# Two index tiles' scores moved into the first attention's first step, a third of the top-k marks moved into the second attention, and GpSimd's low halves written in two operations

## The chip, the cores and the metric

The kernel runs on one core of one Trainium2 chip. The metric is device time in microseconds (us), from the median of several executions. TensorE (PE) multiplies, VectorE (DVE) and ScalarE (ACT) work elementwise on SBUF and PSUM, GpSimd (POOL) splits the weights, SyncE (SP) issues the weight loads. TensorE's granted clock has two levels here, 1.2 and 2.4 GHz (1.00 in the profile).

## The reference, cut to what matters

Two transformer-like layers on 512 tokens of width 1024 are followed by a pooling layer, a dilated-attention layer and a final norm. Each of the first two layers has three branches: an mLSTM, a sparse attention (`_dsa`) in which each query may look only at the 128 keys with the highest index score, and a differential attention (`_diff_attn`).

```python
def _dsa(q, k, v, qi, ki, wi):            # per block of queries
    rel = jax.nn.relu(jnp.einsum('bqhd,bsd->bqhs', qib, ki32))       # 4 index heads
    score = jnp.einsum('bqh,bqhs->bqs', wib * idx_scale, rel)
    score = jnp.where(causal[None], score, -jnp.inf)
    _, idx = lax.top_k(score, topk)                                   # topk = 128
    ...
    s = jnp.where(valid[:, None], jnp.einsum('bqhd,bqkhd->bhqk', qb, k_sel) * (dh ** -0.5), -jnp.inf)
    p = jax.nn.softmax(s, axis=-1)

def _diff_attn(q, k, v, lam):
    p = jax.nn.softmax(jnp.where(causal, s, -jnp.inf), axis=-1)
    a = p[:, :, 0] - lam * p[:, :, 1]
```

## The kernel before, in words

All 512 tokens are resident as four tiles of 128 (`NT` = 4). Every engine has its own program, written by hand, and the engines meet only at semaphores. So the order of the text is the order of each engine's queue.

Weights come in 546 chunks of up to 1024 columns through four `RAW` slots. For each chunk GpSimd (`split`, L371 to L382) writes a rounded high half `WH` (L377) and then the rest, `WL` (L380), into one of two slots; `weights_split` tells TensorE that `WL` is complete, and `chunk_done` frees the slot. TensorE multiplies with `WH` and then with `WL` (`by_columns`, L407). The small operation at L376 is the one on which GpSimd waits for a free slot.

In each of the two layers a stretch of mLSTM work is followed by the index scores, and these by two attentions. The index scores (PE L664, ACT's relu in `RELU`, DVE L1713 to L1720) are made for the query tiles n = 1, 2 and 3, four heads each, with 256, 384 and 512 keys; tile 0 needs none. Four PSUM banks (0, 1, 4, 5) carry the heads, two `RELU` buffers pass them to VectorE, and VectorE adds the weighted heads in the tile's part of `MSK`. Only behind the last relu does ScalarE copy the turned keys (`take` into `SKT` and `DKT`) that the first attention's scores wait for.

The attentions are `for a in range(2)`: a = 0 is the differential one, a = 1 the sparse one. Both run nine steps q = 0 to 8; step q makes the scores of tile n = q // 2 for four heads and finishes step q - 1. TensorE's order in a step of a = 0 is: `scores(q)` (L729), `gate_high` (L691, 16 matmuls), `turn_probs(q-1, 0)` (L740), `gate_low` (L699, 8), `values` (L752), `turn_probs(q-1, 1)`, `branch` (L407, 12), `values`. The gate and branch chunks are the weights of the gated merge; they are placed there to fill TensorE. In a = 1 there are four `turn_probs` and `values` a step, the first `values` directly behind `gate_high`.

VectorE's order in a step is: four masked maxima of the scores (L1776) and their negation (L1781), in a = 0 the normalised difference of the probabilities of q - 1 (L1790 to L1797), `use_gate(q-1)` (L1754), `scale_gate(q)` (L1743), then in a = 0 six rounds of `mark_top`, and in every other step a copy of the attention's output (L1815, or L1818 to L1820). A round of `mark_top` takes the eight highest index scores of a tile (L1730) and overwrites them with a marker (L1731). Sixteen rounds do a tile, and L1733 turns the markers into the mask. The 48 rounds of the three tiles fill the steps 0 to 7 of a = 0. The masks are read by L1776 of a = 1: tile 1's at q = 2, tile 2's at q = 4, tile 3's at q = 6.

ScalarE's order in a step is: four exponentials of q, the copies of the turned probabilities of q - 1 to `TB`, and the gate's tanh.

## Time and profile before

| | us |
|---|---|
| median of 3 runs (lowest 3347.69, highest 3351.09) | 3349.46 |
| the profiled execution | 3356.99 |
| its span, first to last instruction | 3354.8 |
| busy: PE / DVE / ACT / POOL | 3094.3 / 1679.1 / 577.0 / 1872.8 |
| mean granted clock of TensorE | 0.969 |

The span is the profiled execution without 2.2 us around it. An engine's busy time is a mean over stages with different limits, so the stages are to be looked at one by one. In the chain of waits each line is the start, the duration and the work that the end of the program waited for; in a timeline a bracket tells how long the engine had stood idle and who released it.

### The profile page before, as it was taken

To read this page: it belongs to the slowest core of one execution; us is meant where nothing else is said; L and a number is where in the kernel's file an instruction comes from. 1 tells how busy PE (TensorE), PEld (TensorE's weight loads), DVE (VectorE), ACT (ScalarE), POOL (GpSimd) and SP (SyncE) were. 2 spreads that over 40 slices of the span, in tenths; PEclk is the share of its full clock that TensorE was granted. 3 is DMA by queue.
4 is the path that set the end of the run, shared out by engine and by line. 5 is a ranking of instruction groups with operands and counts; after the bars stand their busy time and mean duration, and the time that the engine had idled before them with its cause. 6 is when DMAs were issued, how large, how long until landed. Compare 5 with 4: busy or idle time off the path is not lost.

```text
span 3354.8 us, 39077 instructions
## 1 busy us (share of the span) xinstructions
PE 3094.3 (92%) x14414; PEld 2545.1 (76%) x14414; DVE 1679.1 (50%) x2562; ACT 577.0 (17%) x1130; POOL 1872.8 (56%) x1645
## 2 busy tenths in 40 slices
PE   8977889999999987779999999999999999998998
PEld 6866667788877876557778878777778888887876
DVE  6777853554433777773464433555422223323544
ACT  3223233110001331323110000000011211111000
POOL 5643333666667664324566667665565554444664
PEclk9998999999999998889999999999999999999999
DMA  4321111333323321111233323322222222222322
GB/s 137 95 63 42 56 47 54 116 94 94 102 82 114 103 86 54 47 42 57 65 122 97 97 88 95 94 83 92 85 88 76 82 74 67 67 67 66 97 88 75
DMA packets 86524, 272.49 MB, mean 81 GB/s; under 512 B 9984, under 2 KB 10624, under 8 KB 86400
## 3 DMA queue, kind: packets, MB, share of 16 engines
q1 hardware_dynamic: 86400, 270.84, 26.5%
q8 instruction: 78, 1.28, 0.2%
q14 instruction: 46, 0.38, 0.0%
HBM read 266.61 MB, written 4.19 MB: 81 GB/s over the span
## 4 chain that ended last, share of the span: by engine, by line
PE 81%; DVE 14%; ACT 3%; issue 1%; DMA 0%; SPq 0%; POOL 0%; DVEq 0%; ACTq 0%
PE PS L407 54%; PE PS L456 13%; PE PS L699 3%; PE PS L691 3%; DVE MSK L1731 2%; DVE SMALLS L1730 2%; PE PS L927 2%; PE PS L752 1%; PE PS L953 1%; DVE MS L1776 1%; ACT MS L1042 1%; PE PS L740 1%; PE PS L941 1%; PE PS L420 1%; ACT TB L1042 1%
## 5 line engine op out<-in xcount | busy, mean ns | idle before, releaser
L380 POOL TENSOR_TENSOR WL<-RAW,WH 128x1024 fp32r<-128x1024 f32 (+3 forms) x546 | 1229.1, 2251 | 45.5
L376 POOL TENSOR_TENSOR POOL_C<-POOL_C 128x1 f32<-128x1 f32 x546 | 127.7, 234 | 1412.6 <-PE PS L407 776.5
L407 PE MATMUL PS<-XNH,WH 128*128 128x512 f32 x1752 | 694.0, 396 | 14.2 <-DVE EYL L1428 9.1
L407 PE MATMUL PS<-XNL,WH 128*128 128x512 f32 x1752 | 686.5, 392 | 0.0
L377 POOL TENSOR_SCALAR WH<-RAW 128x1024 fp32r<-128x1024 f32 (+3 forms) x546 | 538.2, 986 | 0.5 <-issue 0.5
L407 PE MATMUL PS<-XNH,WL 128*128 128x512 f32 x1752 | 432.9, 389 | 0.0
L407 PEld LDWEIGHTS PS<-XNH,WH 128*128 128x128 f32 x1752 | 330.7, 189 | 87.1 <-DVE EYL L1428 10.3
L407 PEld LDWEIGHTS PS<-XNL,WH 128*128 128x128 f32 x1752 | 330.7, 189 | 69.2 <-issue 1.0
L407 PEld LDWEIGHTS PS<-XNH,WL 128*128 128x128 f32 x1752 | 328.1, 187 | 69.0
L456 PE MATMUL PS<-WH,XNH 128*128 128x512 f32 (+1 forms) x768 | 288.4, 376 | 6.7 <-ACT TB L1042 3.8
L456 PE MATMUL PS<-WH,XNL 128*128 128x512 f32 (+1 forms) x768 | 285.9, 372 | 0.0
L1970 DVE SCALAR_TENSOR_TENSOR OQK<-PS,RT 128x512 f32<-128x512 f32 x48 | 33.1, 692 | 312.9 <-PE PS L407 307.0
L456 PE MATMUL PS<-WL,XNH 128*128 128x512 f32 (+1 forms) x768 | 178.3, 372 | 0.0
L456 PEld LDWEIGHTS PS<-WH,XNH 128*128 128x128 f32 x768 | 145.0, 189 | 28.4 <-ACT TB L1042 4.4
L456 PEld LDWEIGHTS PS<-WH,XNL 128*128 128x128 f32 x768 | 144.7, 188 | 19.6
L456 PEld LDWEIGHTS PS<-WL,XNH 128*128 128x128 f32 x768 | 141.5, 188 | 20.3
L691 PE MATMUL PS<-XNH,WH 128*128 128x512 f32 x384 | 156.5, 408 | 0.0
L691 PE MATMUL PS<-XNL,WH 128*128 128x512 f32 x384 | 151.2, 394 | 0.0
L407 PE MATMUL PS<-HH,WH 128*128 128x512 f32 x352 | 139.5, 396 | 7.3 <-DVE HL L1428 7.3
L407 PE MATMUL PS<-HL,WH 128*128 128x512 f32 x352 | 139.3, 396 | 0.0
L1845 DVE TENSOR_TENSOR HT<-SILU,PS 128x512 f32<-128x512 f32 x44 | 30.3, 688 | 202.1 <-PE PS L407 199.6
L1428 DVE TENSOR_TENSOR HL<-HT,HH 128x512 f32 (+1 forms) x44 | 112.6, 2559 | 5.1
(351 smaller groups left out, 4713.5 us busy)
## 6 DMA issues: line engine op xcount, KB each, us to landing
RAW<-w_oslot SPq DMA_DIRECT2D x56, 512.0 KB, 3.6
RAW<-w_L0ffn SPq DMA_DIRECT2D x44, 512.0 KB, 3.6
RAW<-w_L1ffn SPq DMA_DIRECT2D x44, 512.0 KB, 3.6
RAW<-w_od SPq DMA_DIRECT2D x32, 512.0 KB, 3.6
RAW<-w_epool SPq DMA_DIRECT2D x24, 512.0 KB, 3.6
RAW<-w_oslot SPq DMA_DIRECT2D x32, 384.0 KB, 3.1
RAW<-w_eug SPq DMA_DIRECT2D x16, 512.0 KB, 3.6
RAW<-w_eout SPq DMA_DIRECT2D x16, 512.0 KB, 3.6
```

Of the source, the lines that this page charges most:

```text
L376: nc.gpsimd.tensor_tensor(POOL_C[:, 1:2], POOL_C[:, 0:1], POOL_C[:, 0:1], ALU.add)
L377: nc.gpsimd.tensor_scalar(WH[:, half, 0:w], RAW[:, slot, 0:w], 1.0, 0.0, ALU.mult, ALU.add).then_inc(S("high_ready"), 1)
L380: nc.gpsimd.tensor_tensor(WL[:, half, 0:w], RAW[:, slot, 0:w], WH[:, half, 0:w].bitcast(F32), ALU.subtract).then_inc(S("weights_split"), 1)
L407: mm = nc.tensor.matmul(bank, w[:, slot, k * cols:(k + 1) * cols], x[:, k0 + k, :], start=first and j == 0 and w is WH and x is hi, stop=l ...
L456: mm = nc.tensor.matmul(outs[n], x[:, k, n * P:(n + 1) * P], w[:, slot, j * cols:(j + 1) * cols], start=k == 0 and w is WH and x is hi, st ...
L691: nc.tensor.matmul(PS[b][:, :], WH[:, c % 2, k * P:(k + 1) * P], x[:, k, :], start=k == 0 and x is XNH, stop=False)
L699: mm = nc.tensor.matmul(PS[b][:, :], WL[:, c % 2, k * P:(k + 1) * P], XNH[:, k, :], start=False, stop=k == KD - 1)
L927: nc.tensor.matmul(PS[g][:, 0:(n + 1) * P - k0], OQK[:, half, g, n * P:(n + 1) * P], OQK[:, half, 3 + g, k0:(n + 1) * P], start=True, stop ...
L1042: nc.scalar.activation(out_, in_, func, **more).then_inc(sem, 1)
L1428: V.tensor_tensor(dst_lo, src, dst_hi.bitcast(F32), ALU.subtract).then_inc(sem, 1)
L1730: then(V.max(TOP8, m))
L1731: then(V.match_replace(m, TOP8, m, TAKEN))
```

## The change

1. `mark_top`: in a = 0, four rounds instead of six in each of the steps 0 to 7 (rounds 0 to 31: tiles 1 and 2). The sixteen rounds of tile 3 go to the steps 0 to 3 of a = 1, four in each, at the same place of VectorE's step.
2. Index scores: only tile 1 is made before the attentions. The scores, relus and sums of the tiles 2 and 3 go into step 0 of a = 0: on TensorE behind `gate_low` and ahead of `branch`, with two banks (4, 7) instead of four; on ScalarE behind the exponentials and ahead of the gate's tanh; on VectorE behind the four rounds of marks. `RELU` lies in `TMP` instead of `SQ`, which holds the gates by then.
3. GpSimd writes the low half of a 1024-column chunk in two operations of 512 columns; the second signals. Narrower chunks are as before.

```diff
-        RELU = SQ
+        RELU = TMP
...
-                nc.gpsimd.tensor_tensor(WL[:, half, 0:w], RAW[:, slot, 0:w],
-                                        WH[:, half, 0:w].bitcast(F32), ALU.subtract
+                if w == 1024:
+                    nc.gpsimd.tensor_tensor(WL[:, half, 0:512], RAW[:, slot, 0:512],
+                                            WH[:, half, 0:512].bitcast(F32), ALU.subtract)
+                at_ = 512 if w == 1024 else 0
+                nc.gpsimd.tensor_tensor(WL[:, half, at_:w], RAW[:, slot, at_:w],
+                                        WH[:, half, at_:w].bitcast(F32), ALU.subtract
                                         ).then_inc(S("weights_split"), 1)
...
-                for n in range(1, NT):
+                def index_scores(n, banks):
+
                     w = (n + 1) * P
                     for h in range(IDX_HEADS):
-                        b = (0, 1, 4, 5)[h]
+                        b = banks[h % len(banks)]
                         claim(b)
...
+                index_scores(1, (0, 1, 4, 5))
                 pe.wait_ge(*L("sk_normed", 1))
...
                         if gated:
                             gate_low(name, i)
+                        if a == 0 and q == 0:
+                            index_scores(2, (4, 7))
+                            index_scores(3, (4, 7))
...
-                act.wait_ge(*L("dk_normed", 1))
-                for n in range(1, NT):
+                def index_relu(n, banks):
+
                     for h in range(IDX_HEADS):
                         i = 4 * (n - 1) + h
                         act.wait_ge(*L("idx_ready", i + 1))
                         if i >= 2:
                             act.wait_ge(*L("idx_used", i - 1))
                         w = (n + 1) * P
-                        run(RELU[:, i % 2, 0:w], PS[(0, 1, 4, 5)[h]][:, 0:w], ACT.Relu, L("relu_ready"))
+                        run(RELU[:, i % 2, 0:w], PS[banks[h % len(banks)]][:, 0:w], ACT.Relu, L("relu_ready"))
+
+                act.wait_ge(*L("dk_normed", 1))
+                index_relu(1, (0, 1, 4, 5))
...
+                        if a == 0 and q == 0:
+                            index_relu(2, (4, 7))
+                            index_relu(3, (4, 7))
...
-                for n in range(1, NT):
+                def index_sum(n):
+
...
+
+                index_sum(1)
...
                         if a == 0 and q < 8:
-                            for r in range(6):
-                                mark_top(6 * q + r)
+                            for r in range(4):
+                                mark_top(4 * q + r)
+                        if a == 0 and q == 0:
+                            index_sum(2)
+                            index_sum(3)
+                        if a == 1 and q < 4:
+                            for r in range(4):
+                                mark_top(32 + 4 * q + r)
```

## Rows read from the trace of the kernel before

**Rows 1.** The page: shares of the chain of waits by engine, whole span.

```profile
PE 81%; DVE 14%; ACT 3%; issue 1%; DMA 0%; SPq 0%; POOL 0%; DVEq 0%; ACTq 0%
```

**Rows 2.** Busy time in two stretches (start:end, length, each engine's busy us, granted clock).

```profile
329.00:447.00 118.00, 91.62 (x423) 70.83 (x421) 100.82 (x284) 26.90 (x78) 45.14 (x48) 0.92 0.19 54
...
465.00:581.00 116.00, 107.12 (x582) 84.67 (x581) 35.16 (x106) 35.30 (x97) 45.52 (x48) 0.99 0.19 55
```

**Rows 3.** Chain of waits, first attention: first and last gate scaling, and marks between.

```profile
329.56 0.69 DVE SQ L1743
...
331.14 0.44 DVE SMALLS L1730
...
332.12 0.44 DVE SMALLS L1730
...
402.34 0.71 DVE SMALLS L1730
...
403.85 0.70 DVE SMALLS L1730
...
434.32 0.69 DVE SQ L1743
```

**Rows 4.** Timeline of TensorE, first attention: a short and two long pauses.

```profile
349.71 2.09 PE L699 MATMUL PS<-XNH,WL 128*128 128x512 f32 x8
...
363.95 0.66 PE L740 MATMUL PS<-IDENT,MS 128*128 128x128 f32 x2 [3.91 <-DVE MS L1797]
...
430.17 0.65 PE L740 MATMUL PS<-IDENT,MS 128*128 128x128 f32 x4 [3.76 <-DVE MS L1797]
430.55 3.66 PE L699 MATMUL PS<-XNH,WL 128*128 128x512 f32 x8
```

**Rows 5.** Timeline of TensorE: last gate_high matmul of two steps, first values of one.

```profile
359.65 0.39 PE L691 MATMUL PS<-XNL,WH 128*128 128x512 f32 x1
...
396.63 0.83 PE L752 MATMUL PS<-DV,TB 128*128 128x128 f32 x6
...
406.61 0.39 PE L691 MATMUL PS<-XNL,WH 128*128 128x512 f32 x1
```

**Rows 6.** Timelines of ScalarE and VectorE, index stretch: relus 4 and 12, a load, sums.

```profile
310.97 0.38 ACT L1042 ACTIVATE SQ<-PS 128x256 f32<-128x256 f32 x1 [0.21 <-DVE MSK L1716]
...
316.80 0.60 ACT L1042 ACTIVATE SQ<-PS 128x512 f32<-128x512 f32 x1 [0.26 <-DVE MSK L1716]
...
321.34 1.28 ACT L1042 ACT_TABLE_LOAD   x1
...
312.42 0.42 DVE L1713 TENSOR_SCALAR MSK<-SQ,SMALLS 128x384 f32<-128x384 f32 x1
...
318.46 0.29 DVE L1720 SCALAR_TENSOR_TENSOR MSK<-CAUSAL,MSK 128x128 f32<-128x128 f32 x1
```

**Rows 7.** Timelines, second attention: VectorE's idle stretches; a copy and its reader.

```profile
469.27 0.29 DVE L1776 CUSTOM_DVE_ANT_0 MS<-PS,CAUSAL 128x128 f32<-128x128 f32 x1 [3.54 <-PE PS L729]
...
491.10 0.20 DVE L1818 RECIPROCAL SMALLS<-SMALLS 128x8 f32<-128x8 f32 x1 [3.37 <-PE PS L752]
...
505.02 0.56 DVE L1776 CUSTOM_DVE_ANT_0 MS<-PS,MSK 128x384 f32<-128x384 f32 x1 [5.19 <-PE PS L729]
...
484.08 0.25 ACT L1042 ACTIVATE TB<-PS 128x128 f32<-128x128 f32 x1
...
484.63 0.33 PE L752 MATMUL PS<-X,TB 128*128 128x64 f32 x2
```

**Rows 8.** Timelines of GpSimd and VectorE side by side, at two ends of a stage.

```profile
649.12 2.39 POOL L380 TENSOR_TENSOR WL<-RAW,WH 128x1024 fp32r<-128x1024 f32 x1
649.35 2.71 DVE L1762 SCALAR_TENSOR_TENSOR ML<-TMP,MH 128x512 fp32r<-128x512 f32 x1
...
1063.81 1.05 POOL L377 TENSOR_SCALAR WH<-RAW 128x1024 fp32r<-128x1024 f32 x1
...
1064.03 1.37 DVE L1417 TENSOR_TENSOR X<-X,HT 128x512 f32<-128x512 f32 x1
1064.95 2.68 POOL L380 TENSOR_TENSOR WL<-RAW,WH 128x1024 fp32r<-128x1024 f32 x1
```

## The prediction

> **What bounds the kernel now.** I read the page's chain of waits first. The end of the program waits for TensorE in 81% of the span and for VectorE in 14%, for GpSimd in none [rows 1]. The 14% are not spread evenly, so I went to the busy times by stretch. In the first attention of layer 0 (329 to 447) VectorE is busy 100.8 of 118 us, TensorE 91.6, at a mean granted clock of 0.92; in the second attention (465 to 581) it is the other way round, VectorE 35.2 of 116 us and TensorE 107.1 at 0.99 [rows 2]. So the first attention waits for VectorE, and the second has VectorE to spare. That is the stage to price. The chain there runs in a ring: scaling the gate (L1743), the marks, the maxima, the difference of the probabilities, then TensorE's `turn_probs` and `gate_low`, then L1743 again. The seven rounds of that ring, from the first L1743 at 329.56 to the last at 434.32, take 104.8 us [rows 3]. TensorE's pauses in it end at a VectorE result, L1797 [rows 4]. Layer 1 repeats the picture, so I price one layer and double it.
>
> **The change part by part.** All sums are in the profiled execution, 3356.99 us, which is 7.5 us over the median of the three runs; I take that off at the end.
>
> *Marks out of the first attention.* A round costs the distance between two L1730: 332.12 - 331.14 = 0.98 us over 256 keys and 403.85 - 402.34 = 1.51 over 512 [rows 3]; for 384 keys I take the middle, 1.25. In the seven ring turns VectorE now does rounds 0 to 41: 16 x 0.98 + 16 x 1.25 + 10 x 1.51 = 50.8 us. Afterwards it does rounds 0 to 27: 16 x 0.98 + 12 x 1.25 = 30.7. That is 20.1 us off a stage in which VectorE ends last. The mask step L1733 of tile 2 also moves out of these turns into the tail; I price it like half a round, 0.7.
>
> *What is late next.* With less to do on VectorE, TensorE's own step could bind. For 256 keys it is from `gate_low` at 349.71 to the last `gate_high` matmul at 359.65 and its 0.23, 10.2 us, and 0.2 for the turn: 10.4 [rows 4, 5]. For 512 keys it is 396.63 to 406.84, 10.2 us, then 0.35 of turns and 1.9 of `gate_low`: 12.4 [rows 4, 5]. For 128 keys the same parts are 9.3: 2.8 of `branch`, 0.7 of scores, 3.7 of `gate_high`, 0.2 and 1.9. VectorE's seven turns would be 104.8 - 20.1 - 0.7 - 4.8 (the clock, next) = 79.2 us, 11.3 in the mean, shorter at first and longer at the end, since the maxima and probabilities grow with the keys. So VectorE stays last but in the first turns; I give back 1.2, an estimate.
>
> *The clock.* After a short pause the eight matmuls of `gate_low` take 2.09 us; after a pause of 3.76 they take 3.66 [rows 4], because the engine is then at the lower of its levels, 1.2 instead of 2.4 GHz. There are three such pauses in the ring of layer 0, at 363.95 the first and at 430.17 the last [rows 4]. Shorter marks leave no pause above 1.5 us in the turns 2 to 7, so 3 x 1.6 = 4.8 us come back.
>
> *Index tiles 2 and 3.* Ahead of the attention they are a serial chain. ScalarE's fourth relu ends at 311.35 and its twelfth at 317.40 [rows 6], and the copies of the keys, the scores and everything else follow the last: 6.0 us less. In step 0 they come back. VectorE's eight sums and two causal adds take 318.75 - 312.42 = 6.3 us [rows 6]. The added wait is TensorE's: its last index matmul needs bank 7, which needs the tenth relu, which needs the eighth sum, and that is queued on VectorE behind the gate scaling (0.7) and four rounds (3.9). From L1743 on, this is 0.7 + 3.9 + 2.7 (the first four sums) + 0.6 (a relu [rows 6]) + 0.5 = 8.4 us until `branch(0)` may start; behind it are queued `scores(1)`, `gate_high(1)` and all that the next turn needs. Then follow the 9.3 from above, and one slow start of 1.7 after the long pause. The first turn is then 19.4 us instead of 9.3. So the move costs 10.1 and returns 6.0: it loses 4.1 us. If the clock stays up it loses 2.4. The trace has no relu behind an exponential; if the change of function asks for a table, there and back, each load costs 1.28 as the one at 321.34 [rows 6], 6.7 us lost; I take 0, since the relus of the trace follow a root without one. The chunk of `branch(0)` keeps its slot 8 us longer, so GpSimd's and SyncE's queues stand for as long; no load or split is moved past another, and both are two chunks ahead when they go on.
>
> *The tail.* Behind the last L1743 stand six rounds of 1.51, afterwards four of 1.25 and a mask step: 9.1 - 5.0 = 4.1, less the moved 0.7 but without TensorE in the way, so 3.7.
>
> The first attention with its approach: 20.1 + 0.7 + 4.8 - 1.2 - 10.1 + 6.0 + 3.7 = 24.0 us a layer.
>
> *Marks into the second attention.* Four rounds of 1.51 are 6.0 us, at a place where VectorE has now idle stretches of 3.54 (behind step 0), about 4, 3.37 and 5.19 us before it is wanted again [rows 7]. They overflow by 2.5, 2.0, 2.7 and (with the mask step) 1.3 us. Behind them wait the maxima, behind these ScalarE's exponentials, and in ScalarE's queue behind those the copy to `TB` that TensorE's first `values` reads. The slack there is small: the copy ends at 484.33 and its reader starts at 484.63 [rows 7]. I take 0.3 to 0.5 off in the first two steps and nothing in the others: 2.0 + 1.6 + 2.7 + 1.3 = 7.6, and 0.6 for a chance of the lower clock after the longest pause: 8.2 us a layer. Bounds: 0 if TensorE's order absorbs it all, and 24 if no round is covered.
>
> *GpSimd in two operations.* VectorE's ML took 2.71 us: it came 0.23 behind the low half's start and ended 0.55 after its end at 651.51, so it stood and then worked [rows 8]. And it gets in between two operations: GpSimd's L377 ended at 1064.86, its next one came 0.09 later, and VectorE's L1417, waiting since 1064.03, was through at 1065.40, while that next operation was drawn out to 2.68 [rows 8]. So two halves cut such a wait by some 1.1 us where VectorE's operation is the last before TensorE goes on; in a row of such operations the second waits for the second half and nothing is won. On the path I count three single ones a layer (this one, and at the starts of the two norms): at 1.1, 1.1 and 0.7 that is 2.9 a layer, 5.8 in all. The mLSTM stretch has rows of them: 0, with +-3 either way. GpSimd's own cost rises by an instruction's start, which I bound by the 0.09 between two operations and 0.5: nothing, since nobody waits for it [rows 1]. That cover is gone only where a chunk's split outlasts TensorE's 24 matmuls on the other slot, 24 x 0.23 = 5.5 us; the split is 1.05 + 0.09 + 2.39 and a small operation, some 3.7 [rows 8].
>
> The Trainium skill, SBUF — State Buffer, section "Who interferes with whom", says the shared port pair is an exclusive lock held for the whole instruction, and that a VectorE instruction with two SBUF inputs contends with a reading GpSimd one. Rows 8 agree. By the rule alone, total blocking is not reduced by cutting an operation, only its longest piece is; a row of contending operations would win nothing, and the sum would be 0 instead of 5.8 if every wait were in such a row.
>
> The sum: 2 x (24.0 - 8.2) + 5.8 = 37.4. 3356.99 - 37.4 = 3319.6, less 7.5 gives 3312 us.
>
> **The rivals.**
> - *The marks hide wholly in the second attention* (each step's slack is larger than the one row shows, since `gate_high` runs meanwhile): 16 us more come off, 3296 us. Against it: the 0.3 us in rows 7.
> - *Half the gain of the first attention.* TensorE, or ScalarE's exponentials ahead of the copies, takes VectorE's place in every turn instead of two: 12 a layer are lost, 3336 us. For it: TensorE's 12.4 us in the late turns, close to what VectorE has left.
> - *The gains cancel.* Besides that, the clock drops in each of the four second-attention steps (4 x 1.6 = 6.4 a layer), 2 x (12.0 - 8.2 - 6.4) + 5.8 = 0.6, 3349 us: no difference.
> - *Slower, by one mechanism: the marks in the second attention are fully exposed.* The place is the wait for the maxima; the price is 4 x (6.0 + 1.6 for the clock) + 0.7 = 31 us a layer against 24, so 14 more in all and 3349.5 + 14 - 6 = 3358. It decides from (24.0 + 2.9) / 4 = 6.7 us a step upward. Against it: VectorE's idle stretches are in the trace, 3.4 us and more.
> - *The port's gain is larger*: the stretched waits of the mLSTM stretch are halved as well, some six a layer at 1.1: 3299 us.
> - *It doesn't do what it says*: if tile 3's marks were not done before step 6 reads them the step would wait; they end in step 3, so I give this nothing.
>
> **How the numbers follow.** The forecast, 3312 (3300 to 3326 by its own terms), has 0.55; marks hidden 0.10; larger port gain 0.08; half the gain 0.15; cancelled 0.07; slower 0.05. The range for 8 in 10 takes in both rivals below and half the gain above: 3292 to 3338. A difference of 0.2%, 6.7 us, is about what a measurement of this kernel can tell from none. Faster by more: 0.55 + 0.10 + 0.08 + 0.15 = 0.88; within: 0.07; slower: 0.05.
>
> **What would show it.** In the profile after: L1743 of the first attention some 89 to 92 us from first to last instead of 104.8, with a first turn of 18 to 20 and the others at 10 to 13; granted clock above 0.95 there; the first scores 6 us earlier; TensorE idle 1.3 to 2.7 us before `values` in the steps 1 to 4 of the second attention, released by ScalarE; GpSimd's low halves of 1024 columns gone, ML near 1.6. I am wrong if TensorE waits for GpSimd anywhere, if turns 3 to 7 stay above 14 us, or if the clock falls in the second attention.

## The result and the profile after

The changed kernel takes 3326.15 us (median of 4 runs, 3320.76 to 3331.25), the kernel before in the same comparison 3348.71: a ratio of 0.9922, 95% interval 0.9911 to 0.9934. The medians differ by 22.6 us, the ratio makes it 26 with an interval of 22 to 30; 37.4 was forecast. The kernel is faster, by some 0.7 to 0.8%. The profiled execution took 3326.61, 30.4 less than the one before.

**The chain of waits.** The page of the changed kernel, shares of the span by engine:

```profile
PE 83%; DVE 12%; ACT 3%; issue 1%; DMA 0%; SPq 0%; POOL 0%; DVEq 0%; ACTq 0%
```

VectorE's share went from 14 to 12% [rows 1]. The busy times by stretch say where (start:end, length, busy us of PE, PEld, DVE, ACT, POOL, then the granted clock). The stretches are the first turn of the first attention's ring, its other six turns, and the steps 0 to 3 of the second attention:

```profile
326.06:349.17 23.11, 19.62 (x65) 11.84 (x65) 13.69 (x40) 6.79 (x18) 5.78 (x8) 0.78 0.11 34
349.17:418.93 69.76, 68.50 (x342) 52.93 (x340) 60.08 (x184) 23.26 (x66) 34.63 (x42) 1.00 0.24 68
442.40:505.23 62.83, 53.57 (x251) 41.48 (x250) 41.54 (x107) 18.09 (x60) 23.18 (x28) 0.89 0.17 51
```

In the six other turns TensorE is busy 68.5 of 69.8 us at the full clock. In the kernel before the same six turns took 93.9 us, with TensorE busy in 76.0 of them at 0.91:

```profile
340.44:434.32 93.88, 75.97 (x341) 58.20 (x340) 79.40 (x221) 23.16 (x66) 33.83 (x36) 0.91 0.18 51
```

The price stands in the other two rows of the changed kernel: a first turn of 23 us at a clock of 0.78, and four steps of the second attention at 0.89 (1.00 in layer 1, below).

**The first turn.** Timeline of VectorE, changed kernel; the gate scaling is now L1762, a round of marks L1749 and L1750, an index sum L1730 and L1733, a maximum L1795:

```profile
326.06 0.69 DVE L1762 TENSOR_TENSOR SQ<-PS,RT 128x512 f32<-128x512 f32 x1 [4.66 <-PE PS L706]
...
330.59 0.42 DVE L1730 TENSOR_SCALAR MSK<-TMP,SMALLS 128x384 f32<-128x384 f32 x1
331.12 2.06 DVE L1733 SCALAR_TENSOR_TENSOR MSK<-TMP,SMALLS,MSK 128x384 f32<-128x384 f32 x3
...
335.11 0.75 DVE L1733 SCALAR_TENSOR_TENSOR MSK<-TMP,SMALLS,MSK 128x512 f32<-128x512 f32 x1 [0.80 <-ACT TMP L1052]
...
343.18 0.29 DVE L1795 CUSTOM_DVE_ANT_0 MS<-PS,CAUSAL 128x128 f32<-128x128 f32 x1 [4.23 <-PE PS L736]
```

TensorE in the same stretch (L669 is an index score, two records for each head; L411 is `branch`):

```profile
327.44 1.29 PE L669 MATMUL PS<-X 64*128 64x384 f32 x4 [0.57 <-ACT TMP L1052]
331.65 5.55 PE L669 MATMUL PS<-X 64*128 64x512 f32 x8 [2.91 <-ACT TMP L1052]
337.13 0.79 PE L411 MATMUL PS<-YAH,WH 128*128 128x512 f32 x1
...
342.55 0.71 PE L736 MATMUL PS<-DKT,DQT 64*128 64x128 f32 x8
```

TensorE stands 2.91 us behind the marks, then does tile 3's four heads in 5.55 us, 1.39 a head, at a low clock, and `branch` after them is slow too, 5.42 us from 337.13 to 342.55. VectorE, whose sums should be the slow part, waits between them.

**The second attention.** TensorE's waits before `values` (L759) and one `gate_low` (L706) behind them; VectorE's last round of marks and the maxima behind it; the copy to `TB`:

```profile
455.95 0.66 PE L759 MATMUL PS<-X,TB 128*128 128x64 f32 x2 [2.75 <-ACT TB L1052]
...
456.48 3.76 PE L706 MATMUL PS<-XNH,WL 128*128 128x512 f32 x8
...
485.80 0.97 PE L759 MATMUL PS<-X,TB 128*128 128x64 f32 x4 [2.69 <-ACT TB L1052]
...
502.39 0.66 PE L759 MATMUL PS<-X,TB 128*128 128x64 f32 x4 [1.60 <-ACT TB L1052]
```

```profile
452.11 0.68 DVE L1750 MATCH_REPLACE8 MSK<-SMALLS,MSK 128x512 f32<-128x512 f32 x1
452.82 0.29 DVE L1795 CUSTOM_DVE_ANT_0 MS<-PS,CAUSAL 128x128 f32<-128x128 f32 x1
...
455.55 0.26 ACT L1052 ACTIVATE TB<-PS 128x128 f32<-128x128 f32 x1
```

The maxima have no idle time in front of them now, where [rows 7] had 3.54 us: they start when the marks end. The exponentials, the copy and `values` follow in the order that the prediction named.

Layer 1 has the same pause of 2.75 us at the same place, and there the clock stays up: `gate_low` takes 2.09 us, and the four steps take 59.1 us instead of 62.8. The same steps in the second profile of the kernel before (*before again*, layer 0) are the last row:

```profile
1490.41 0.41 PE L759 MATMUL PS<-X,TB 128*128 128x64 f32 x2 [2.75 <-ACT TB L1052]
...
1490.69 2.09 PE L706 MATMUL PS<-XNH,WL 128*128 128x512 f32 x8
...
1476.73:1535.80 59.07, 48.12 (x251) 36.94 (x250) 41.53 (x107) 18.22 (x60) 23.22 (x28) 1.00 0.18 54
...
465.04:515.53 50.49, 47.68 (x251) 37.10 (x250) 19.01 (x57) 18.28 (x60) 22.57 (x24) 1.00 0.20 63
```

**GpSimd's halves.** GpSimd and VectorE at `ML` (L1781 now):

```profile
640.26 1.31 POOL L381 TENSOR_TENSOR WL<-RAW,WH 128x512 fp32r<-128x512 f32 x1
...
641.54 1.73 POOL L384 TENSOR_TENSOR WL<-RAW,WH 128x512 fp32r<-128x512 f32 x1
...
640.50 1.63 DVE L1781 SCALAR_TENSOR_TENSOR ML<-TMP,MH 128x512 fp32r<-128x512 f32 x1
```

VectorE stands behind one half, gets in between the two and ends at 642.13, 0.56 after the first half's end, against 2.71 us and 0.55 in [rows 8].

Stage by stage, from the two profiles (us, after less before, from the same instructions; the ring is first to last gate scaling, the head is from the first index sum to the first gate scaling, the tail from the last gate scaling of the first attention to the first of the second):

| stage | layer 0 | layer 1 | forecast |
|---|---|---|---|
| head | -7.5 | -6.0 | -6.0 |
| ring: 104.76 to 92.87, 105.78 to 92.88 | -11.9 | -12.9 | -14.3 |
| tail | -2.6 | -4.1 | -3.7 |
| second attention, steps 0 to 3 | +10.3 | +8.6 | +8.2 |
| sum | -11.7 | -14.4 | -15.8 |

The rest of the 30.3 us by which the spans differ, 4.2, lies outside these stages, where 5.8 were forecast.

### The profile page after: what moved, and what is told of

Its sections match the earlier page's. It is cut to its first block, busy times and chain, and to the rows that moved or that the text cites. A ratio compares the mean times of both kernels' runs of the same rounds, so it can differ in the third digit from the quotient of the medians.

```text
span 3324.5 us, 39485 instructions
## 1 busy us (share of the span) xinstructions
PE 3092.5 (93%) x14414; PEld 2542.7 (76%) x14414; DVE 1595.8 (48%) x2562; ACT 577.3 (17%) x1130; POOL 1993.3 (60%) x2041
## 4 chain that ended last, share of the span: by engine, by line
PE 83%; DVE 12%; ACT 3%; issue 1%; DMA 0%; SPq 0%; POOL 0%; DVEq 0%; ACTq 0%
PE PS L411 54%; PE PS L460 13%; PE PS L698 3%; PE PS L706 3%; PE PS L759 2%; PE PS L937 2%; PE PS L963 1%; DVE MSK L1750 1%; ACT MS L1052 1%; DVE SMALLS L1749 1%; DVE MS L1795 1%; PE PS L424 1%; PE PS L747 1%; PE PS L951 1%; PE PS L736 1%
## 5 line engine op out<-in xcount | busy, mean ns | idle before, releaser
L384 POOL TENSOR_TENSOR WL<-RAW,WH 128x512 fp32r<-128x512 f32 (+2 forms) x546 | 824.7, 1511 | 12.5
L411 PE MATMUL PS<-XNH,WH 128*128 128x512 f32 x1752 | 694.5, 396 | 14.6 <-DVE EYL L1444 9.5
L411 PE MATMUL PS<-XNL,WH 128*128 128x512 f32 x1752 | 686.8, 392 | 0.0
L381 POOL TENSOR_TENSOR WL<-RAW,WH 128x512 fp32r<-128x512 f32 x396 | 541.6, 1368 | 33.1
L411 PE MATMUL PS<-XNH,WL 128*128 128x512 f32 x1752 | 432.8, 389 | 0.0
L411 PEld LDWEIGHTS PS<-XNH,WH 128*128 128x128 f32 x1752 | 331.1, 189 | 87.2 <-DVE EYL L1444 10.7
L411 PEld LDWEIGHTS PS<-XNL,WH 128*128 128x128 f32 x1752 | 331.1, 189 | 69.2 <-issue 1.0
L411 PEld LDWEIGHTS PS<-XNH,WL 128*128 128x128 f32 x1752 | 328.2, 187 | 69.1
L411 PE MATMUL PS<-HH,WH 128*128 128x512 f32 x352 | 139.1, 395 | 7.3 <-DVE HL L1444 7.3
L411 PE MATMUL PS<-HL,WH 128*128 128x512 f32 x352 | 138.7, 394 | 0.0
```

The source lines that it names most:

```text
L381: nc.gpsimd.tensor_tensor(WL[:, half, 0:512], RAW[:, slot, 0:512], WH[:, half, 0:512].bitcast(F32), ALU.subtract)
L384: nc.gpsimd.tensor_tensor(WL[:, half, at_:w], RAW[:, slot, at_:w], WH[:, half, at_:w].bitcast(F32), ALU.subtract).then_inc(S("weights_spli ...
L411: mm = nc.tensor.matmul(bank, w[:, slot, k * cols:(k + 1) * cols], x[:, k0 + k, :], start=first and j == 0 and w is WH and x is hi, stop=l ...
```

## The experiments

All are complete kernels; `before_again` is the kernel before itself. Ratios are to the kernel before in the same comparison.

### Each part by itself

*Halves alone* keeps this part of the diff and drops the rest; *no halves* does the opposite:

```diff
+                if w == 1024:
+                    nc.gpsimd.tensor_tensor(WL[:, half, 0:512], RAW[:, slot, 0:512],
+                                            WH[:, half, 0:512].bitcast(F32), ALU.subtract)
```

> Third part alone: GpSimd's low halves of 1024 columns in two operations, marks and index tiles as before. My theory (a single contending VectorE operation that TensorE waits for gets in 1.1 us earlier, three of them a layer, rows of such operations win nothing): 5.8 us less than before, with the wait for ML near 1.6 us instead of 2.7. Rival: in the mLSTM stretches the rows of contending operations lose, as the +4.0 us of layer 0's stretch in the changed kernel suggests, so that the whole is between 0 and 4 us slower than before.

Measured: 3348.2 against 3355.34, 0.998 (0.9971 to 0.9989): 6.7 us less, interval 3.7 to 9.7. TensorE's waits for `ML` and for `XNL` at a norm, halves alone:

```profile
651.65 0.50 PE L411 MATMUL PS<-MH,WH 128*128 128x512 f32 x1 [1.70 <-DVE ML L1778]
...
1066.53 0.50 PE L424 MATMUL PS<-XNH,WH 128*128 128x512 f32 x1 [2.26 <-DVE XNL L1399]
```

In the kernel before the same two waits were 2.64 and 2.97 us. So single waits are 0.9 and 0.7 us shorter. More of it shows over a longer stretch, from the last gate scaling (L1743) of layer 0 to tile 1's causal add in layer 1; it holds `ML`, the norm and layer 1's mLSTM work. It takes 718.6 to 720.9 us in the six profiles with whole low halves and 711.7 to 716.0 in the eight with halves, 5.3 less in the mean. The single waits are a part of this only; which other waits fell is not taken apart here. Behind layer 1's last gate scaling nothing shows (1662.2 and 1661.9 us to the end in the mean, with 1658 to 1665 in single profiles).

> Parts one and two (marks and index tiles) with GpSimd's low halves whole. By my theory the halves are worth 5.8 us, so this kernel is 5.8 us slower than the changed kernel, 3332, and its gain on the kernel before is 17 us, all of it in the two attentions. Rival (halves lose in rows of contending operations): it is as fast as the changed kernel or up to 4 us faster, 3322 to 3326.

Measured: 3334.45, 0.9935 (0.9921 to 0.9948), 20.9 us less than the median beside it where the changed kernel has 22.6; by the ratios, 0.0013, the difference is 4.4, and the intervals overlap. So by its time this run neither adds to the run of the halves alone nor speaks against it; in the stretch from layer 0 to layer 1 it has 720.0 us, the changed kernel 715.9. The +4.0 us of layer 0's mLSTM stretch, which had made me think of the rival, was nothing that the halves do: in layer 0 the first index tile's causal add starts at 313.8 to 316.1 us in the eight profiles with halves (mean 314.6) and at 312.1 to 317.1 in the six without (mean 314.8). The first profile of before, with 312.1, was the earliest of all.

*Marks alone* leaves `index_scores`, `index_relu` and `index_sum` for tiles 1 to 3 ahead of the attention; *index alone* keeps six rounds a step in the first attention:

```diff
-                            for r in range(4):
-                                mark_top(4 * q + r)
+                            for r in range(6):
+                                mark_top(6 * q + r)
...
-                        if a == 1 and q < 4:
-                            for r in range(4):
-                                mark_top(32 + 4 * q + r)
```

> Part one alone: four rounds of marks a step in the first attention and sixteen in the second's first steps, index tiles all ahead of the attention as before, low halves whole. My theory: 20.8 (rounds and mask step) + 4.8 (clock) - 1.2 + 3.7 (tail) less the 9.4 us that the second attention was seen to lose, 18.7 us a layer, 37 us less than before: about 3311, which is faster than the changed kernel by some 15 us, since its first turn was 23.1 us. Rival: the index move is worth its place, that is, without it the first turns of the ring keep VectorE and TensorE in each other's way, and this kernel gains no more than the changed one, 3326 or above.

Measured: 3320.54, 0.989 (0.9875 to 0.9905): 37 us less than before, as my theory had it, and better than the changed kernel by a ratio of 0.0032, 11 us; the two intervals, up to 0.9905 and from 0.9911, do not overlap. The whole ring, marks alone:

```profile
330.94:410.69 79.75, 78.16 (x387) 60.13 (x386) 69.18 (x214) 25.81 (x76) 39.42 (x42) 1.00 0.23 70
```

Its first turn is 9.47 us (9.23 in layer 1).

> Part two alone: index scores, relus and sums of tiles 2 and 3 in the first attention's step 0, marks six a step there as before, low halves whole. My theory: the first scores come 6 to 7 us earlier and the first turn of the ring is lengthened by more than that (six rounds of marks, 5.9 us, now stand ahead of the sums instead of four), to 25 us from some 14.5: slower than before by 2 x (10.5 - 6.5) = 8 us, 3357. Rival: the sums fall where VectorE waits anyway, and the kernel gains up to 6 us a layer, 3337.

Measured: 3369.89, 1.0038 (1.0024 to 1.0051): slower than before by 12.7 us. The first turn is 23.8 and 23.7 us (10.9 before), and from tile 1's causal add to the first gate scaling it is 10.0 instead of 17.5 and 16.0: the move costs 12.9 and returns 6.8 a layer in the mean, which makes 12.2 in all. This settles the second part: it loses by itself (+12.7) as it does on top of the marks (0.9935 against 0.989, +15).

### Why the first turn is so long

*Sums first* puts VectorE's index sums ahead of the step's marks (low halves whole):

```diff
+                        if a == 0 and q == 0:
+                            index_sum(2)
+                            index_sum(3)
                         if a == 0 and q < 8:
                             for r in range(4):
                                 mark_top(4 * q + r)
-                        if a == 0 and q == 0:
-                            index_sum(2)
-                            index_sum(3)
```

> As no_halves (parts one and two), but in step 0 of the first attention VectorE does the index sums of tiles 2 and 3 ahead of its four rounds of marks. My theory: the first turn of 22.5 us is long since the sums stand behind the marks, and TensorE's index matmuls, which need banks that these sums set free, then start from a pause at the lower clock. Then the turn falls by 4 to 5 us to some 18, and the kernel is 8 to 10 us faster than no_halves. Rival: TensorE, ScalarE and VectorE hand eight tiles round with two buffers, and the length is that chain's own; then the marks only move behind it, and the turn stays within 1.5 us of 22.5.

Measured: 3327.17, 0.9906 (0.9891 to 0.9921), not clearly apart from *no halves*. The stage is clear: the first turn is 20.4 us in both layers instead of 22.4 and 22.6. I had expected 4 to 5 us off, the rival under 1.5; 2.1 came. TensorE, sums first:

```profile
325.34 1.29 PE L666 MATMUL PS<-X 64*128 64x384 f32 x4 [0.58 <-ACT TMP L1049]
326.83 1.12 PE L666 MATMUL PS<-X 64*128 64x512 f32 x2 [0.20 <-ACT TMP L1049]
329.03 4.40 PE L666 MATMUL PS<-X 64*128 64x512 f32 x6 [1.08 <-ACT TMP L1049]
```

Even with the marks gone from between, the eight heads need 9.5 us, from 323.85 to 333.4. At the full clock their matmuls would take some 4.1 us (in the next experiment two heads over 384 keys take 0.92, two over 512 take 1.13). TensorE, ScalarE and VectorE hand a tile round with two buffers, and TensorE waits. From 329.03 to 333.36 its mean clock is 0.55: the last three heads take 4.40 us and are part of the chain themselves. The marks in the middle are 2 us of it, the chain the larger part.

*Index in pairs* keeps all three parts, but gives out the heads two by two:

```diff
+        PAIRS = {0: (2, (0, 1)), 1: (2, (2, 3)), 3: (3, (0, 1)), 5: (3, (2, 3))}
...
-                        if a == 0 and q == 0:
-                            index_scores(2, (4, 7))
-                            index_scores(3, (4, 7))
+                        if a == 0 and q in PAIRS:
+                            index_scores(PAIRS[q][0], (7, 4), PAIRS[q][1])
```

(VectorE's sums likewise; ScalarE's relus stand behind the first copy to `TB` of the step.)

> As the changed kernel (all three parts), but the eight index tiles of token tiles 2 and 3 go two by two into steps 0, 1, 3 and 5 of the first attention instead of all into step 0, so that none of them waits for a sum. My theory: the first turn's 23.1 us is that of a chain of eight and falls to 11 or 12, each of the four steps pays some 1 us on TensorE, and the ring goes from 92.9 to 83 or 84 us while the head keeps its 6.5 us: 17 to 19 us less than the changed kernel and 2 to 5 less than marks_halves. Rival: each pair makes TensorE wait for a relu and then for a copy queued behind it, 3 us a step or more; then it is no faster than marks_halves.

Measured: 3317.76, 0.9869 (0.9854 to 0.9884). The turns are 10.88, 12.51, 10.43, 13.28, 12.33, 15.50 and 13.18, the ring 88.1. So the ring got 4.8 us shorter a layer, but is 4 to 5 us longer than the 83 or 84 expected. The ratio is 0.0053 (18 us) better than the changed kernel's, in the 17 to 19 expected, but the stages do not show that much: the two profiled executions, 3321.93 and 3326.61, are 4.7 us apart. But against the same kernel with all tiles ahead (*marks and halves*, below, ring 79.06) the ring is 9.0 us longer, and the way from tile 1's causal add to the first gate scaling is 10.0 us instead of 19.0 and 16.0: nothing gained in one layer, 3 us lost in the other. In this stage TensorE is already busy in 77.8 of 79.1 us (*marks and halves*). The eight heads add 5.5 us to its busy time and 3.5 to its pauses. One pair, and the wait behind it:

```profile
334.63 0.92 PE L670 MATMUL PS<-X 64*128 64x384 f32 x4
336.12 0.49 PE L760 MATMUL PS<-DV,TB 128*128 128x128 f32 x2 [0.58 <-ACT TMP L1052]
```

The rival, that it is no faster than all tiles ahead, holds; its price of 3 us or more a step was too high, the four turns with a pair are 1.6, 2.3, 2.0 and 3.1 us longer.

### The marks in the second attention

*Marks and halves* is the changed kernel without the second part.

> Parts one and three, index tiles all ahead of the attention. From the single runs: marks alone 0.989 of before, halves 0.998 or (changed kernel against no_halves) 0.9987. If the parts add up, 0.987 to 0.988: 41 to 43 us less than before and some 16 us less than the changed kernel. Rival: halves and marks help the same waits of VectorE; then 0.989 as marks_only.

Measured: 3313.33, 0.9868 (0.9853 to 0.9883), 46 us less than the 3359.61 of its comparison. The parts add up. The steps 0 to 3 of the second attention still take 61.4 to 63.8 us, 50.5 in the kernel before.

*Places* lays the sixteen rounds of tile 3 in twelve places instead of four:

```diff
+                PRE, POST, done = (1, 1, 1, 2, 2, 2), (1, 1, 1, 1, 1, 2), [32]
...
+                        if a == 1 and q < 6:
+                            marks_of(PRE[q])
                         if q:
                             use_gate(gates_of, p)
...
-                        if a == 1 and q < 4:
-                            for r in range(4):
-                                mark_top(32 + 4 * q + r)
+                        if a == 1 and q < 6:
+                            marks_of(POST[q])
```

> As marks_halves, but tile 3's sixteen rounds in the second attention are laid in twelve places instead of four: one or two ahead of each step's combination of the gate and one or two behind its scaling, over steps 0 to 5. In the kernel before VectorE idles there 3.2 to 5.2 us at both places of each step, and no place now gets more than 3.0 us. My theory: the 8.6 to 10.3 us that steps 0 to 3 lost come back but for 1 or 2: 14 to 18 us less than marks_halves. Rival: the delayed gate is what TensorE or ScalarE then waits for, since the gate's scaling and combination stand behind the added rounds; then less than 8 us come back.

Measured: 3299.37, 0.9823 (0.981 to 0.9837), 14 us less than *marks and halves* beside it, at the lower end of the 14 to 18 expected. Steps 0 to 3, places:

```profile
433.08:482.91 49.83, 46.86 (x244) 36.33 (x243) 32.98 (x88) 17.51 (x56) 22.54 (x27) 1.00 0.21 64
```

49.8 us (51.3 in layer 1), the 50.5 of the kernel before, with ten of the sixteen rounds in it. One stands ahead of them, and the next three turns, up to step 7, hold the other five and take 62.4 us, 62.2 in the kernel before. VectorE still waits for TensorE behind most of the places:

```profile
456.83 0.69 DVE L1759 TENSOR_TENSOR SQ<-PS,RT 128x512 f32<-128x512 f32 x1 [2.02 <-PE PS L707]
...
469.00 0.69 DVE L1759 TENSOR_TENSOR SQ<-PS,RT 128x512 f32<-128x512 f32 x1 [1.00 <-PE PS L707]
...
475.00 0.56 DVE L1799 CUSTOM_DVE_ANT_0 MS<-PS,MSK 128x384 f32<-128x384 f32 x1 [3.92 <-PE PS L737]
```

So the 11 to 13 us a layer that *marks and halves* lost there (50.5 to 61.4 and 63.8) were the overflow of four rounds over one idle stretch and its consequences, and not the rounds as such. In the medians 14 us came back.

### How many rounds the first attention bears

With four rounds a step VectorE still idled 0.8 to 1.8 us ahead of the gate scalings of the ring. If that is slack, TensorE is last in every turn. Both runs change the counts only (48 rounds in all):

```python
# rounds in the steps 0 to 7 of a = 0; in the steps 0 to 5 of a = 1, ahead of use_gate and behind scale_gate
# places: four in each;              PRE, POST = (1, 1, 1, 2, 2, 2), (1, 1, 1, 1, 1, 2)
FIRST_ = (3, 3, 3, 3, 3, 3, 3, 3);   PRE, POST = (2, 2, 2, 2, 2, 2), (2, 2, 2, 2, 2, 2)   # three
FIRST_ = (5, 5, 5, 5, 5, 5, 5, 5);   PRE, POST = (0, 0, 1, 1, 1, 1), (0, 0, 1, 1, 1, 1)   # five
```

> As marks_halves_places, but three rounds of marks a step in the first attention instead of four, and the eight taken out laid with the sixteen in the twelve places of the second attention, two in each. If VectorE is still last in most turns of the first attention, as the prediction has it, seven rounds of 0.98 to 1.25 us and a mask step go from the ring: 8 us a layer, and 2 in the tail, 20 us less than marks_halves_places. If TensorE is last in all of them since four a step (it waits 0.31 and 0.77 us in the whole ring of marks_only), the ring stays at 78 to 79 us and only the tail gives some 2 us a layer: 4 to 5 us less.

> Five rounds a step in the first attention, the other eight in eight places of steps 2 to 5 of the second. VectorE waits 0.9 to 1.8 us for TensorE in each turn with four rounds. If that is slack, a fifth round of 0.98 to 1.25 us is nearly free in the turns 1 to 6, the last turn and the tail pay for rounds over 512 keys and the mask step: ring 81 to 82 us, in all 7 to 10 us more than marks_halves_places. If VectorE's rounds are on the path as they stand, the ring gets 10 us longer, 20 to 24 us more in all.

Measured: three 3299.58, 0.982 (0.9789 to 0.9851); five 3325.95, 0.9915 (0.9897 to 0.9934). The ring, three and then five rounds a step:

```profile
333.25:410.52 77.27, 77.27 (x387) 60.53 (x386) 61.59 (x194) 26.19 (x76) 40.28 (x49) 1.00 0.23 72
...
334.61:424.76 90.15, 80.07 (x387) 61.16 (x386) 78.42 (x236) 25.79 (x76) 40.44 (x49) 0.98 0.20 62
```

| rounds a step | ring, us | from | 
|---|---|---|
| six, low halves whole | 105.7 | kernel before, second profile, both layers |
| six | 103.7 and 104.2 | halves alone, layers 0 and 1 |
| five | 90.2 | both layers |
| four | 79.1 | places, both layers |
| three | 77.3 | both layers |

The seven turns of layer 0 (*three*, *places* and *five*):

| rounds a step | turn 1 | 2 | 3 | 4 | 5 | 6 | 7 |
|---|---|---|---|---|---|---|---|
| three | 9.3 | 10.2 | 10.3 | 11.3 | 11.4 | 12.4 | 12.5 |
| four | 9.3 | 10.2 | 10.4 | 11.3 | 12.3 | 12.4 | 13.2 |
| five | 9.9 | 10.5 | 11.4 | 13.6 | 13.6 | 13.5 | 17.7 |

At three TensorE is busy in the whole of the ring: its floor, as the second of the two cases of the expectation had it (77.3 against 78 to 79). The 4 to 5 us that this was to give in all do not show: 0.982 against 0.9823 for *places*, with a wide interval. At five the first case, slack, failed: it gave 81 to 82 us and 90.2 came. The second held: 11 us more in the ring for 10, and by the ratios 31 us more than *places* in all (26 more than *three* beside it) for 20 to 24. Five of TensorE's pauses with five rounds are behind VectorE's probabilities and above 0.9 us; four of them:

```profile
364.05 0.41 PE L748 MATMUL PS<-IDENT,MS 128*128 128x128 f32 x2 [0.91 <-DVE MS L1821]
...
377.62 0.41 PE L748 MATMUL PS<-IDENT,MS 128*128 128x128 f32 x2 [2.12 <-DVE MS L1821]
...
391.07 0.52 PE L748 MATMUL PS<-IDENT,MS 128*128 128x128 f32 x3 [2.00 <-DVE MS L1821]
...
420.72 1.08 PE L748 MATMUL PS<-IDENT,MS 128*128 128x128 f32 x4 [3.56 <-DVE MS L1821]
```

VectorE's idle time ahead of the gate scaling is for the most part no slack: VectorE waits there for `gate_low`, which waits for the turn of VectorE's own probabilities. The wait is a link of the ring. With five rounds it is 0.9 to 1.1 us in six of the seven turns, though VectorE is last there; with four it is 0.8 to 1.8, with three, where TensorE is last, 0.9 to 2.0. From six (*halves alone*, layer 0) to five the ring lost 13.6 us: VectorE's busy time in it went from 87.7 to 78.4, and its idle time, which the low clock behind the long pauses had drawn out, from 16.0 to 11.7. From five to four rounds worth 9.5 us went (40.2 to 30.7, by the 0.98, 1.25 and 1.51 of the prediction) and a mask step of 0.9, and 11.1 were measured. From four to three seven rounds of 1.25 go, 8.8 us, and 1.8 are gained. So at four rounds the ring stands 1.8 us above TensorE's floor.

### The tail

In *places* TensorE still waits behind the last marks: they and the mask step hold VectorE from 409.61 to 415.5, and

```profile
417.27 0.64 PE L748 MATMUL PS<-IDENT,MS 128*128 128x128 f32 x4 [3.38 <-DVE MS L1820]
```

*Tail free* moves them on:

```python
# places: four in each;              PRE, POST = (1, 1, 1, 2, 2, 2), (1, 1, 1, 1, 1, 2)
FIRST_ = (4, 4, 4, 4, 4, 4, 4, 0);   PRE, POST = (1, 1, 2, 2, 2, 2), (1, 1, 2, 2, 2, 2)   # tail free
```

> As marks_halves_places, but none of the marks in the first attention's last step: its four rounds and the mask step (5.9 us on VectorE, in front of the last probabilities, while TensorE idles 3.38 us) go to the second attention, 20 rounds in the twelve places, one or two in each. Expected by the row on that idle stretch: 3.4 us a layer and up to 1.5 for the lower clock behind it, so 7 to 10 us less than marks_halves_places. Rival: the tail's length is that of the heads' copy, the roots and the norm behind it, and TensorE only waits later: under 3 us less.

Measured: 3287.23, 0.98 (0.9766 to 0.9834), the lowest median of all, 12 us below *three* beside it (7 by the ratios) and by the ratios 8 below *places*, for 7 to 10 expected. The intervals of the three overlap, so the times alone do not show it. The stage does: the tail is 18.27 us in both layers (24.1 and 23.5 in *places*), with the clock at full:

```profile
412.90:431.17 18.27, 15.91 (x99) 13.13 (x98) 14.49 (x32) 8.59 (x17) 9.01 (x10) 1.00 0.14 45
```

5.2 to 5.8 us a layer, above the 3.4 to 4.9 expected. In *places* the matmuls behind that pause ran slower, a clock of 0.79 over layer 0's tail.

### The kernel before once more

> The kernel before once more, for a second profile. The profiled execution on which the prediction rests was some 8 us over its median. If these 8 us lie in the stretches of the mLSTM and of the waits on GpSimd, the ring is again 104 to 106 us and the rest is shorter. If they lie in the attentions, the ring or the second attention's first steps are 2 to 4 us shorter a layer than in the first profile, and the gain that the profiles showed there was too large by as much.

Measured: 3359.64. The ring is 105.7 in both layers and steps 0 to 3 of the second attention 50.5 in both. The 52.55 of layer 0 in the first profile stands alone, with a clock of 0.97 there. So neither of my two readings holds: the ring is the same, and so is the attention but for those 2 us. The execution on which the prediction rests was simply a usual one: the medians of this kernel were 3355.3, 3359.6 and 3356.2 in the three later comparisons, and 3349 in the first.

## Why the prediction was right, and where its sizes were off

**The stage.** That in the kernel before VectorE bounds the first attention and TensorE the second is what the runs show. 3326.15 lies in the range of 3292 to 3338, just outside the forecast's own 3300 to 3326. No rival came: the marks did not hide wholly (they cost 9 to 12 us a layer), half the gain was not lost in the ring, the clock did not eat it all. Of the signs, the other turns (10.2 to 13.2), `ML` at 1.63 and the waits of 2.75, 2.69 and 1.60 us before `values` came, and TensorE waits for GpSimd only at the very start, as before. The ring (92.9 for 89 to 92), its first turn (23.1 for 18 to 20) and its clock (0.94 for above 0.95) missed. One sign of being wrong came: the clock fell in the second attention, in layer 0 (0.89), not in layer 1 (1.00).

**Marks out of the first attention: the sum right, its reason in part.** Rounds 20.1, mask step 0.7, clock 4.8, less 1.2: a ring of 80.4 without the index tiles. *Marks alone* has 79.75 and 79.49. But the step "VectorE stays last but in the first turns" failed, and the sum came out because the two engines are so close. TensorE's own turns, by the prediction's figures (9.3, twice 10.4, two between 10.4 and 12.4, twice 12.4), add up to 77.7 us against 79.2 for VectorE; measured, TensorE's floor is 77.3. With four rounds TensorE is last in the turns 1, 2, 4 and 6, which are as long as with three, and VectorE clearly in 5 and 7 only. TensorE took VectorE's place in most turns, as the rival of half the gain had it, but the ring was not 12 us longer for it. The reading of "three such pauses" in the ring of layer 0 misses a fourth, 3.26 us at 394.42; the `gate_low` behind it took 2.09 us, so three slow starts and the 4.8 us stand.

**The first turn: mis-sized by 3.7 us a layer.** 19.4 were forecast, 23.1 came in both layers. `branch(0)` was to start 8.4 us behind the gate scaling and started 11.1 behind it (326.06 to 337.13). The step that failed is "0.7 + 3.9 + 2.7 + 0.6 + 0.5": it follows VectorE's sums and one relu and puts TensorE's matmuls at nearly nothing. After the pause of 2.91 us they take 1.39 a head and end the chain themselves. The other 0.9 is `branch`, 2.6 us slower than at the full clock where 1.7 were taken. The six other turns, 69.76, were 1.3 below the 71.1 of the sum, so the ring missed by 2.4 us in layer 0 and 1.4 in layer 1 only. That this part loses was right, its size too small: 4.1 us a layer forecast, 6.4 by *index alone* (12.7 / 2) and 7.5 by the ratios of *no halves* and *marks alone* (0.0045).

**The second attention: right mechanism, one size off.** The overflow was taken as 7.6, the clock as 0.6. Against the second profile of before (50.49) layer 1 lost 8.6 us and layer 0 12.3, for the 8.2 forecast. In layer 1 the clock stayed up and the loss is waits: TensorE's pauses in the four steps are 10.95 us instead of 2.73, 8.2 more. So the overflow was right. In layer 0 the pauses are 9.26, 6.5 more, and TensorE's busy time for the same 251 matmuls is 53.57 instead of 47.68, 5.9 us at the low clock. This is the term that was too small, at 0.6. The length of a pause does not settle it: the pauses of 2.75 and 2.69 us are there in both layers, with `gate_low` at 3.76 and 3.23 us behind them in layer 0 and at 2.09 in layer 1, and in the kernel before 2.09 came behind a pause of 3.26 too. A pause of this size is a risk, which the prediction priced at one small chance. What decides between the two is not shown by these runs.

**Halves: right.** 5.8 forecast, 6.7 (3.7 to 9.7) measured alone. Single waits fell by 0.9 and 0.7 where 1.1 and 1.1 or 0.7 were taken. The split into three such waits in each layer does not show in the stages: 5.3 us lie between layer 0's last gate scaling and layer 1's index scores, and nothing shows ahead of layer 0's index scores (314.6 against 314.8) nor behind layer 1's last gate scaling, where the profiles spread over 7 us. That the total agrees is in part luck. The Trainium skill, SBUF — State Buffer, section "Who interferes with whom", has the shared pair as an exclusive lock for a whole instruction; the `ML` row agrees, since VectorE ended 0.56 us after the first of the two halves.

**The index relus behind the exponentials.** Taken at 0 for table loads; the ScalarE timeline shows no load between 326 and 345. The Trainium skill, ScalarE: Activation LUTs, says that cheap functions such as relu are in every table set. The trace agrees.

**The 7.5 us off at the end: wrong.** The profiled execution of before stood 7.5 over its median and I took the same off the forecast. The changed kernel's stands 0.5 over its own, and 3357 was within the usual times of before. That is 7.0 of the 14.2 us by which 3312 missed 3326.15. The other 7.0 (3319.6 to 3326.61) are 2 x 2.75 in the attentions (-13.05 in the mean of the layers for -15.8) and 1.6 in the rest.

## What to carry to other kernels

Move work into idle time only in pieces that fit each idle stretch: sixteen rounds in four places cost 9 to 13 us a layer, the same in twelve cost nothing that shows. An idle wait inside a ring can be a link of it and no slack; change the count by one both ways to see who bounds (five, four and three rounds: 90, 79 and 77 us). When a chain between engines is moved, count the matmuls in it at the clock that the waits leave them, and move no work onto a stage that its engine already fills.

## What was not expected of the hardware

Behind a pause of 2.75 us on TensorE eight matmuls took 3.76 us in layer 0, at the lower of its two clock levels, and 2.09 in layer 1, at the full one. So the same pause can cost or not cost, and two layers of one execution can differ by 4 us for it. In *tail free*, where VectorE's last probabilities come earlier, they fall beside GpSimd's splits, and one operation of 0.75 us took 1.66; it ended 0.55 us after GpSimd's half (414.22 to 415.56):

```profile
414.45 1.66 DVE L1821 SCALAR_TENSOR_TENSOR MS<-MS,SMALLS 128x512 f32<-128x512 f32 x1
```

The tail was shorter all the same. Pauses and the clock also differ where nothing in a change touches them: from tile 1's causal add to the first gate scaling *marks and halves* needs 19.0 us and *places*, with the same code there, 16.1. TensorE's first scores, in that order:

```profile
324.19 1.22 PE L737 MATMUL PS<-DKT,DQT 64*128 64x128 f32 x8 [2.52 <-ACT DKT L1050]
```

```profile
323.50 0.71 PE L737 MATMUL PS<-DKT,DQT 64*128 64x128 f32 x8 [1.36 <-ACT DKT L1050]
```

And tile 1's causal add stood at 312.1 to 317.1 us in fourteen profiles whose code up to there differs only in GpSimd's halves and in the tile that `RELU` lies in, so one pair of profiles can't tell a change of 4 us in that stretch.
